# Sums of squares of the attention heads by two products of rounded parts

## The reference, cut to what matters

```
def _rms(x, w):
    xf = x.astype(jnp.float32)
    y = xf * lax.rsqrt(jnp.mean(xf * xf, axis=-1, keepdims=True) + EPS)
    return (y * w.astype(jnp.float32)).astype(x.dtype)
...
    qh = _rms(q.reshape(b, S, ATTN_HEADS, ATTN_HEAD_DIM).astype(f32), q_norm_w)
    kh = _rms(k.reshape(b, S, ATTN_HEADS, ATTN_HEAD_DIM).astype(f32), k_norm_w)
```

## Time and profile before

| | |
|---|---|
| median of three runs | 2811.4 us (2809.68 to 2814.97) |
| span of the profiled execution | 2812.1 us |
| PE busy | 2702.2 us, 96% |
| DVE, ACT, POOL busy | 1542.3, 1236.4, 996.7 us |
| stage of the change, blocks 0 to 3 | 306.6 to 534.8 us of the span |

### The profile page before, as it was taken

The page is one execution under the profiler, slowest core; times in us unless marked ns, Lnnn a source line. Parts: engine busy times, 40 slices in busy tenths (PEclk is TensorE's granted clock), DMA queues, the critical chain, the costliest instruction groups (busy, mean ns, idle before and its releaser), DMA issues.

```text
span 2812.1 us, 39176 instructions
## 1 busy us (share of the span) xinstructions
PE 2702.2 (96%) x15660; PEld 2245.0 (80%) x15660; DVE 1542.3 (55%) x3011; ACT 1236.4 (44%) x2159; POOL 996.7 (35%) x729
## 2 busy tenths in 40 slices
PE   7999999999999999999999999999999999999997
PEld 5787778778788888879877878667898878888785
DVE  5776680344836778760387341355537238652683
ACT  6454354543124222242388344544533236453682
POOL 4524564314544454433323323100423320143422
PEclk9999999999999999999999999999999999999998
DMA  6406643202334566531200221001222230233102
GB/s 270 151 31 247 230 153 112 74 21 101 135 105 165 221 222 217 184 116 63 104 7 2 105 90 56 34 1 61 76 76 75 105 128 12 71 115 118 46 2 75
DMA packets 54292, 293.71 MB, mean 104 GB/s; under 512 B 4512, under 2 KB 8928, under 8 KB 24288
## 3 DMA queue, kind: packets, MB, share of 16 engines
q1 hardware_dynamic: 24672, 174.07, 17.6%
q10 hardware_dynamic: 29440, 117.14, 11.2%
HBM read 268.10 MB, written 17.86 MB: 102 GB/s over the span
## 4 chain that ended last, share of the span: by engine, by line
PE 61%; DVE 7%; ACT 3%; issue 2%; POOL 1%; DMA 0%; ACTq 0%; DVEq 0%; POOLq 0%
PE psum L478 15%; PE psum L480 15%; PE psum L479 15%; PE psum L2017 3%; PE psum L2064 2%; PE psum L2075 2%; PE psum L4063 2%; PE psum L1821 2%; PE psum L1844 2%; PE psum L1825 1%; PE psum L1833 1%; POOL w_lo L465 1%; DVE pair_row L2035 1%; DVE pair_prob L2044 1%; DVE c_decay L4181 1%
## 5 line engine op out<-in xcount | busy, mean ns | idle before, releaser
L465 POOL TENSOR_TENSOR w_lo<-raw,w_hi 128x512 fp32r<-128x512 f32 x612 | 859.2, 1436 | 1479.1 <-ACT w_hi L473 1479.1
L478 PE MATMUL psum<-a_hi,w_hi 128*128 128x512 f32 (+2 forms) x1880 | 706.7, 376 | 17.0 <-POOL w_lo L465 7.1
L479 PE MATMUL psum<-a_lo,w_hi 128*128 128x512 f32 (+2 forms) x1880 | 688.0, 366 | 0.0
L480 PE MATMUL psum<-a_hi,w_lo 128*128 128x512 f32 (+2 forms) x1880 | 687.8, 366 | 0.0
L478 PEld LDWEIGHTS psum<-a_hi,w_hi 128*128 128x128 f32 (+1 forms) x1880 | 354.2, 188 | 91.5 <-issue 11.1
L479 PEld LDWEIGHTS psum<-a_lo,w_hi 128*128 128x128 f32 (+1 forms) x1880 | 354.5, 189 | 62.7 <-issue 6.4
L480 PEld LDWEIGHTS psum<-a_hi,w_lo 128*128 128x128 f32 (+1 forms) x1880 | 354.1, 188 | 59.3
L473 ACT ACTIVATE w_hi<-raw 128x2048 fp32r<-128x2048 f32 x153 | 292.4, 1911 | 196.7 <-DMA raw<-stream 148.7
L478 PE MATMUL psum<-w_hi,a_hi 128*128 128x256 f32 (+1 forms) x608 | 197.7, 325 | 1.8 <-POOL w_lo L465 1.6
L479 PE MATMUL psum<-w_lo,a_hi 128*128 128x256 f32 (+1 forms) x608 | 193.1, 318 | 0.0
L480 PE MATMUL psum<-w_hi,a_lo 128*128 128x256 f32 (+1 forms) x608 | 192.9, 317 | 0.0
(11 more groups left out here) (486 smaller groups left out, 4706.4 us busy)
## 6 DMA issues: line engine op xcount, KB each, us to landing
raw<-stream SPq DMA_DIRECT2D x153, 1024.0 KB, 4.9
ada_ring<-ada ACTq DMA_DIRECT2D x64, 1024.0 KB, 5.8
x_in<-xres ACTq DMA_DIRECT2D x3, 3072.0 KB, 10.2
ada_ring<-ada SPq DMA_DIRECT2D x8, 1024.0 KB, 21.4
xres<-x_in ACTq DMA_DIRECT2D x3, 2048.0 KB, 6.9
partner<-gq ACTq DMA_DIRECT2D x4, 1024.0 KB, 9.8
xres<-x_in ACTq DMA_DIRECT2D x1, 3072.0 KB, 9.7
own_raw<-stream SPq DMA_DIRECT2D x3, 1024.0 KB, 4.8
```

The costliest lines, as they stand in the source:

```text
L465: last = pool.tensor_tensor(k.lo_of(s)[:, cols], k.raw_of(s)[:, cols], k.hi_of(s)[:, cols].bitcast(F32), ALU.subtract)
L478: pe.matmul(out, lhs[0], rhs[0], start=start, stop=False)
L479: pe.matmul(out, lhs[0], rhs[1], start=False, stop=False)
L480: return pe.matmul(out, lhs[1], rhs[0], start=False, stop=stop)
```

## The change

ACT squares every tile twice: once into an fp32 tile as before, once into a tile of the rounded type (F32R), the high part. POOL subtracts the high part from the fp32 square in place, and gets the low part. PE multiplies both parts by a matrix of ones of the rounded type into one accumulation, two matmuls in place of one. The matrix is copied once by DVE at the end of the first norm. PE no longer waits for ACT's square, but for POOL's part (`norm_parted`). POOL's low parts of weights and of squares go in one written order.

```
-            act.activation(self.squares[:, t % 2], self.qkv[:, t, :], ACT.Square).then_inc(self.squared.sem, 1)
+            act.activation(self.squares[:, t % 2], self.qkv[:, t, :], ACT.Square)
+            act.activation(self.high[:, t % 2], self.qkv[:, t, :], ACT.Square).then_inc(self.squared.sem, 1)
...
-            pe.wait_ge(self.squared.sem, self.squared.at(t))
+            pe.wait_ge(self.parted.sem, self.parted.at(t))
...
-            pe.matmul(k.psum[:, 6 + (t - 1) % 2, :], k.cst("ones"), self.squares[:, (t - 1) % 2], start=True,
-                      stop=True).then_inc(self.summed.sem, 1)
+            out = k.psum[:, 6 + (t - 1) % 2, :]
+            pe.matmul(out, k.ones_r[:], self.high[:, (t - 1) % 2], start=True, stop=False)
+            pe.matmul(out, k.ones_r[:], self.low[:, (t - 1) % 2], start=False, stop=True).then_inc(self.summed.sem, 1)
+
+    def parts(self, pool, t):
+        pool.wait_ge(self.squared.sem, self.squared.at(t + 1))
+        pool.tensor_tensor(self.low[:, t % 2], self.squares[:, t % 2], self.high[:, t % 2].bitcast(F32),
+                           ALU.subtract).then_inc(self.parted.sem, 1)
...
+            for item in (0, "w", 1, 2, "w", 3, 4, "w", 5, "w", "w"):
+                if item == "w":
+                    low_part(k, pool, k.low_made)
+                    k.low_made += 1
+                else:
+                    side.parts(pool, item)
...
+        dve.wait_ge(k.sem_named("consts_loaded").sem, 16)
+        dve.tensor_copy(k.ones_r[:], k.cst("ones"))
```

More of the change, by code:

```diff
@@ L333, in __init__ @@
         self.eps = at("eps", o, [P, 1])
-        o += 4
+        o = (o + 4 + 63) // 32 * 32
+        self.ones_r = at("ones_r", o, [P, P], F32R)
+        o += 4 * P
         assert o <= self.ARENA, o
@@ L445, in pauses, with weight_stream @@
     return at + [N_SLOTS]
-def weight_stream(k, block):
-    first, until = k.low_made, min(x for x in pauses() if x > k.low_made)
+def weight_stream(k, block, until=None):
+    first, until = k.low_made, until or min(x for x in pauses() if x > k.low_made)
     k.low_made = until
@@ L1594, with __init__ @@
 class HeadNorms(Side):
-    def __init__(self, k, block, qkv, rows_of, v_before, squares, rstd, weights):
+    def __init__(self, k, block, qkv, rows_of, v_before, squares, high, low, rstd, weights):
         self.k, self.qkv, self.rows_of, self.v_before = k, qkv, rows_of, v_before
-        self.squares, self.rstd, self.weights = squares, rstd, weights
+        self.squares, self.high, self.low, self.rstd, self.weights = squares, high, low, rstd, weights
+        self.parted = k.sem_named("norm_parted")
         self.tile_free = k.tile_free.base
@@ L1650, in over @@
     def over(self):
-        for x in (self.squared, self.summed, self.logs, self.rooted, self.normed):
+        for x in (self.squared, self.parted, self.summed, self.logs, self.rooted, self.normed):
             x.stage_over(6)
@@ L2147, in dilated_attention @@
     squares = k.at("squares", rest, [P, 2, S])
+    squares_low = k.at("squares_low", rest, [P, 2, S], F32R)
+    squares_high = k.at("squares_high", rest + 28672 + 128, [P, 2, S], F32R)
     rstd = k.at("rstd", rest + 4096, [P, 6, S])
@@ L2163, in norms @@
         return HeadNorms(k, block, qkv[:, j], v_rows[:, (j - 1) % 2] if j else None, values(j - 1) if j else None,
-                         squares, rstd, (q_weight[:], k.col("k_norm_w")))
+                         squares, squares_high, squares_low, rstd, (q_weight[:], k.col("k_norm_w")))
     ada = k.ada.group(12, B0 + 36864, B0 + 61440, rest + 20480, 3, new_rows=True)
@@ L2192, in _ @@
                 act.wait_ge(ada.used, ada.used_at(ada.end))
+        @block.gpsimd
+        def _(pool):
+            for item in (0, "w", 1, 2, "w", 3, 4, "w", 5, "w", "w"):
[4 more added lines that the diff above has]
+                    side.parts(pool, item)
         dense(k, block, [f"qkv{j}"], tiles, act_tile=take, ada=ada.of((8, 4)[j]) if j < 2 else None, barrier=False,
@@ L2201, in dilated_attention @@
         side.over()
+    weight_stream(k, block)
     rows_in = k.tile_free.at(0)
@@ L2422, in first_block @@
     first_norm(k, block, first_ada, x1, a, A0 + 131072)
-    weight_stream(k, block)
+    weight_stream(k, block, SECTIONS["qkv0"][0] + 2)
     other_constants(k, block)
```

## The result

| | median of the runs | runs | profiled span | the stage |
|---|---|---|---|---|
| before | 2810.8 us | 4 | 2812.1 us | 228.04 us |
| after | 2823.7 us (2820.2 to 2829.3) | 4 | 2818.4 us | 240.26 us |

The account below looks back on a forecast made before the run. Blocks 0 and 1 hang on a DVE, ACT and POOL chain, blocks 2 and 3 on PE. Lost 13.5, gained 2.2, clock 1.7: 13.0 us more, 2824.4 us; 8-in-10 range 2815.5 to 2832.

Parts of the forecast that it names:

- Price of the product: On PE: an fp32 product costs 0.90 us, two rounded matmuls 0.45, saving 0.45 us in each of 24 products.
- The fourth rival: On PE: two rounded matmuls cost the fp32 price, so nothing is saved; 2830 us, chance 0.02.
- Second square: On ACT: squaring each tile again takes 0.53 us, delaying by that the vectors DVE needs to begin block 0.
- Product 3 of block 0: PE's squares product for tile 3 waits 8.9 us for POOL's part behind w3 and comes 9.1 us late.
- The first rival: Parts come in time everywhere because POOL is idle half of block 0; all savings count, 2800.6 us, chance 0.07.
- Product 5: Block 0: its part stands behind w4 on POOL, ends at 361.5, and PE's product comes 14.2 us late.
- What a POOL piece costs DVE: Beside ada products each POOL piece takes 2.22 us instead of 1.26, and DVE loses 1.09 us.
- Turn of block 1: End of block 0: waits for w5 and the value copy go, and PE enters the next block 10.8 us late.
- Block 1: Product 1 comes 14.2 us late behind w6, w7 and parts; five products save 2.3; 13.5 us lost at its end.
- The clock: One stretch at granted clock 0.50, behind product 1 of the second block, lasts 3.4 us and costs 1.7 us.
- Blocks 2 and 3: POOL is alone: products 3 and 5 wait 1.6 us together, so each block gains 1.1 us, two gain 2.2.
- The waits in all: Over the stage: PE, or its weight load, waits for POOL's squares_low by some 25 us, mostly in two or three places.

Follow-up runs that it names:

- experiment 1: Kernel before plus ACT's second square, which nobody reads; no POOL parts, fp32 product kept: 2811.5 us beside 2812.0, ratio 0.9998, stage +0.5 us.
- experiment 2: Changed kernel with POOL's parts made but unused; PE multiplies fp32 squares without waiting for parts: 2819.7 us, 1.0031 of before, stage +5.9 us.
- experiment 5: Changed kernel with the change only in blocks 2 and 3, parts on POOL in its order: 2809.1 us, 0.9993 of before, stage -1.9 us.
- experiment 8: Change in blocks 2 and 3 only, POOL's parts placed between pieces of weight low parts: 2808.2 us, 0.9985 of before, stage -4.8 us.
- experiment 6: Change in blocks 2 and 3 only, with the parts made by DVE instead of POOL: 2806.9 us, 0.9984 of before, stage -5.2 us.
- experiment 3: Changed kernel without POOL's parts; PE multiplies the high part twice: 2803.3 us, 0.9971 of before, stage -6.6 us.
- experiment 7: Changed kernel, all blocks, POOL's parts between the pieces of weight low parts: 2817.8 us, 1.0022 of before, stage +6.3 us.
- experiment 4: Changed kernel with parts of 64 of 512 columns, same places and waits, high part multiplied twice: 2818.7 us, 1.0025 of before, stage +7.8 us.

## Why the prediction was right

The mechanism was that of the forecast, and the sum, 13.0 us, lies within 0.8 of the stage and 0.1 of the medians; with four runs a side the 0.1 is luck. One count in it was wrong, of the parts that meet DVE, and runs through three of the points below.

- **Price of the product: right.** From 447.95 to 453.85 it is 5.90 us between two products of block 2, 6.35 before: 0.45 saved each. The fourth rival is out.
- **Second square: right.** ACT's timeline has it 0.53 us behind the first, and experiment 1 measured 0.5 in all:

```profile
311.77 0.63 ACT L1618 ACTIVATE squares<-qkv 128x512 f32<-128x512 f32 x1
312.30 0.62 ACT L1619 ACTIVATE squares_high<-qkv 128x512 fp32r<-128x512 f32 x1
...
345.84 1.91 ACT L475 ACTIVATE w_hi<-raw 128x2048 fp32r<-128x2048 f32 x1 [6.46 <-DVE ada_temp L963]
```

- **Product 3 of block 0: right.** Forecast 8.9 us of wait and 9.1 late; it waited 8.31 and is 8.94 late (39.04 us from the stage's start against 30.10). w3 began 2.66 us later (2.7) and took 8.79 (8.87). The first rival needed part 3 to end before 336.9; it ended at 344.3, and that stage had begun 1.3 us earlier.
- **Product 5: mis-sized by 1.3 us.** Forecast 14.2 late, measured 12.9. The step that failed is "by then DVE has lost 0.53 + 4 x 1.09 = 4.9 us": slot 4's rounding (345.84, above) is only 3.63 us later against the start than in the earlier trace rows, and w4 with it. That is 0.53 + 3 x 1.09 = 3.8: one part too many, for part 4, the second of the pair at 342.10, held up the ada product at 345.35 (row below), the 17th, and the load waits for 16. By the end of the block I had counted six parts. It was five: part 0 ran from 313.00 in 1.31 us, before the first ada product. Experiment 2 measured the delay at 5.9, and 0.53 + 5 x 1.09 is 6.0.
- **What a POOL piece costs DVE: right.** Ada products beside w3 follow at 2.21 us (2.23 before); the first two run while PE waits for part 3. On the side: POOL's 33.53 us on 17 pieces in block 0 of before are 1.97 us each, 1.6 times block 2's 1.26 and not "twice"; the sum went by the timeline's 2.22, so nothing hangs on that word.

```profile
338.74 2.27 DVE L963 SCALAR_TENSOR_TENSOR ada_temp<-ada_ring,ada_rows 128x1024 f32<-128x1024 f32 x1
...
340.95 2.27 DVE L963 SCALAR_TENSOR_TENSOR ada_temp<-ada_ring,ada_rows 128x1024 f32<-128x1024 f32 x1
...
345.35 2.29 DVE L963 SCALAR_TENSOR_TENSOR ada_temp<-ada_ring,ada_rows 128x1024 f32<-128x1024 f32 x1
```

- **Turn of block 1: +10.6, forecast 10.8**, by errors that nearly cancel there: 1.3 too much from product 5, 1.7 too little from the clock behind it (below), and 0.5 too much because the two waits that went had cost PE more than their brackets (see blocks 2 and 3). From product 5 to the turn PE takes 21.62 us, 19.97 without the clock's 1.65, and the forecast's subtraction had left 20.47. The waits for w5 and for the value copy went, as said: DVE's last ada product ended at 374.56, ahead of the turn at 380.51. In block 0 experiment 2's 5.9 us and PE's waits are not added to each other; the longer one covers the other.
- **Block 1: product 1 is 12.9 late (14.2).** Its POOL chain starts at the value copy, which I had put 7.1 us later, for six parts; it came 69.91 us after the start, 6.0 later than in the earlier trace rows. The block ends 14.1 late, where 13.5 and the 1.7 of the clock make 15.2.
- **The clock: one stretch on the path, as counted, and a little of another.** The stretches at 0.50 in the stage after, columns as before, answer to the earlier trace rows:

```profile
339.60:349.80 10.20, 5.41 (x13) 4.25 (x14) 10.20 (x11) 1.91 (x1) 8.94 (x5) 0.50 0.42 157
360.10:363.40 3.30, 3.30 (x17) 3.30 (x17) 3.30 (x5) 0.00 (x0) 3.30 (x2) 0.50 0.15 62
397.60:401.00 3.40, 3.39 (x8) 2.71 (x9) 3.40 (x5) 0.69 (x1) 3.40 (x2) 0.50 0.00 0
```

  The first was hidden as forecast: 5.4 us of work at 0.50 cost half of that, 2.7, and with the 1.3 above they shortened product 5's wait, 2.42 us where 4 to 6 were expected. The second, behind product 5, put off the turn by 1.7, which I had overlooked; then product 1 of block 1, waiting 4.94 us for POOL, swallowed most of it. POOL's chain starts there at the copy at 375.26, and that had waited for PE; DVE alone would have let it go at about 375.0 (in the trace of before the copy began 0.42 us behind the last ada product's end at 370.07), so some 0.3 us came through:

```profile
375.26 0.60 ACT L2199 ACTIVATE v_rows<-psum 128x512 f32<-128x512 f32 x1 [3.15 <-PE psum L482]
```

  The third, behind product 1, is the one that I counted: from product 1 to product 2 it is 7.63 us, where 5.90 are usual, so it cost 1.7. The stretch of before had cost nothing: block 1 takes the same in two experiments that leave it as it was, one with its clock at 1.00 (experiment 5) and one at 0.97 (experiment 8). PE's busy time is 1.6 us longer in the second, and the block 0.02. In experiment 5 PE waits 1.62 us for a low part of weights (first row); in experiment 8 that wait is not there:

```profile
378.52 0.50 PE L480 MATMUL psum<-a_hi,w_hi 128*128 128x512 f32 x1 [1.62 <-POOL w_lo L467]
```
```profile
369.92:428.00 58.08, 55.98 (x280) 45.62 (x281) 40.24 (x46) 29.55 (x37) 39.78 (x23) 1.00 0.35 126
```
```profile
369.90:428.00 58.10, 57.58 (x280) 46.91 (x281) 40.26 (x46) 29.55 (x37) 39.79 (x23) 0.97 0.36 126
```

- **Blocks 2 and 3: -0.9 each (-1.1)**, with waits of 0.25 and 0.84 at products 3 and 5, where 1.6 was expected for both together. The brackets are not the whole price: block 2 of experiment 6, where no product waits, is 1.64 us shorter (52.86 against 54.50), 1.09 of that in PE's idle time and 0.55 in its busy time. So the 1.6 was right, and what is short is the saving, 2.6 us and not 2.7 in a block without waits.
- **The waits in all: 20.5 us (some 25).** Product 5 is short by 2 to 3 us. The 25 was also more than the forecast's own list, whose middles (8.5, 5, 5 and twice 1.5) add up to 21.5.

The price of the parts, 18.8 us by experiment 3, divides so when the place is taken away first. Placing them behind whole low parts costs 5.9 us (the change against experiment 7), half in blocks 2 and 3 (3.0) and half in blocks 0 and 1. DVE's delay in block 0 costs 5.4 (experiment 2 against 1). The remaining 7.5 are nearly all in block 1, where experiment 7 takes 7.3 us longer than experiment 3; PE's 6.4 us of waits for parts stand there, and a clock of 0.95 instead of 1.00. How they share these 7.3 us was not separated, since no run kept the waits without the fall of the clock behind them. In block 0 another order gives other shares: with short parts, which all but take away DVE's delay (experiment 4), the block still loses 7.0 us, and with the place gone (experiment 7) 5.9. Each alone makes more than half of the block's 10.6, so that mending one gives back less than it costs by itself.

## What to carry to other kernels

Before work is given to an idle engine, look in which stretch it is idle and what its neighbour does there: POOL's 31 us of spare time in block 0 lay beside ada products that made each of its instructions 1.7 times as long. Then look at what stands ahead of the new work in that engine's queue, since a part of 1.3 us behind four pieces of 2.2 us arrives 9 us late, and put it between the pieces or on the engine that has nothing else to do. One edit made in four blocks is four changes: here it paid only in the two where PE alone had set the time.

## What the runs showed of the hardware

- A POOL instruction of 128x64 took 0.33 us alone and 1.29 to 1.34 beside two-input DVE products of 1.22, which were held up by only 0.12 (one part, which met just the end of a product, took 0.53); one of 128x512 took 1.31 and 2.25, and held them up by 1.07. An eighth of the columns took about an eighth of the time from DVE, but still more than half of the time of POOL.
- The granted clock was at 0.50 for 3.3 and 3.4 us behind PE's waits of 2.42 and 4.94 us, and for 10.2 at the wait of 8.31: for the last 4.8 of that wait and 5.4 of the work behind it. Of these the one behind product 1 of block 1 cost 1.7 us; the others only shortened the next wait, but for some 0.3 us.
- Outside the stage, in code that both kernels share, the ten profiled executions took 2578.0 to 2585.1 us. One profile of each kernel can therefore be 6 us off in its span, half of the effect looked for here, while the stage alone agreed with the medians within about 2.
